# A decoder-layer kernel on one core: one level of Strassen on all projections but v and o

## The reference

```python
z = xn @ w_in                      # 1024 -> 7 * 1024: u, v, b_gate, c_gate, x_in, r_a, r_b
u, v = gelu(u), layer_norm(gelu(v))
y_a = (u * chunk_spatial_mix(v, w_s, b_s)) @ w_a_out
c_in = c_gate * x_in
y_b = (b_gate * short_conv(c_in, conv_w)) @ w_b_out     # causal, three taps
h = sigmoid(r_a) * y_a + sigmoid(r_b) * y_b
x1 = x + rms_norm(h @ w_o)
f = (silu(xn1 @ w_gate) * (xn1 @ w_up)) @ w_down        # xn1 = rms_norm(x1); hidden width 2816
y = x1 + rms_norm(f)
```

## Time and profile before

| | |
|---|---|
| median of 3 runs | 1787.79 us (1787.73 to 1787.82) |
| profiled execution: its own time | span 1785.2 us, from the first to the last instruction |
| TensorE, matmul (PE) | 1740.3 us, 97% of the span, 10888 matmuls |
| TensorE, weight loads (PEld) | 1712.0 us, 96% |
| VectorE (DVE) | 565.0 us, 32% |
| ScalarE (ACT) | 366.2 us, 21% |
| GpSimd (POOL) | 416.5 us, 23% |
| mean granted TensorE clock | 0.990 of 2.4 GHz |

### The profile page before, as it was taken

One profiled execution on the slowest core, in us unless ns is written; L12 is line 12 of the kernel. 1 busy time (PEld: TensorE's weight loads), 2 busy tenths in 40 slices (PEclk: granted clock), 3 DMA queues, 4 the chain that ended last, 5 costly groups with the idle time before them and its releaser, 6 DMA issues.

```text
span 1785.2 us, 25730 instructions
## 1 busy us (share of the span) xinstructions
PE 1740.3 (97%) x10888; PEld 1712.0 (96%) x10888; DVE 565.0 (32%) x720; ACT 366.2 (21%) x459; POOL 416.5 (23%) x211
## 2 busy tenths in 40 slices
PE   8999999999999999999888899999999999999997
PEld 6889999999999999999888899999999999999997
DVE  7645420001322322111446932122122122121225
ACT  5212211111111111111433321111111111111136
POOL 2001122222212122222644322222222112222215
PEclk9999999999999999999998999999999999999999
DMA  7221111111111111111330111111111111111102
GB/s 252 70 72 36 35 48 47 46 40 45 47 47 47 47 47 48 47 47 47 104 98 13 36 36 48 47 44 47 38 47 47 47 47 47 47 47 47 48 25 96
DMA packets 145598, 96.89 MB, mean 54 GB/s; under 512 B 5092, under 2 KB 136292, under 8 KB 145556
## 3 DMA queue, kind: packets, MB, share of 16 engines
q1 hardware_dynamic: 133808, 91.34, 16.6%
q10 hardware_dynamic: 11748, 4.95, 1.0%
HBM read 87.75 MB, written 8.56 MB: 54 GB/s over the span
## 4 chain that ended last, share of the span: by engine, by line
PE 91%; DVE 7%; ACT 2%; issue 0%; DMA 0%; DVEq 0%; POOL 0%; SPq 0%
PE ps L449 88%; DVE g L1332 1%; DVE tmp L1323 1%; PE ps L532 1%; DVE xt L1318 1%; DVE g L1317 1%; DVE tmp L1301 1%; PE ps L741 0%; PE ps L708 0%; DMA g<-in_w_in 0%; DVE op_lo L1112 0%; PE ps L623 0%; PE ps L479 0%; DVE xn_lo L1260 0%; ACT g L964 0%
## 5 line engine op out<-in xcount | busy, mean ns | idle before, releaser
L365 POOL TENSOR_TENSOR ring_lo<-stage,ring_hi 128x1024 fp32r<-128x1024 f32 x129 | 310.3, 2406 | 1228.7 <-ACT ring_hi L859 1226.6
L449 PE MATMUL ps<-xn_hi,ring_hi 128*128 128x344 f32 x2208 | 481.5, 322 | 3.9 <-DVE xn_lo L1341 3.2
L449 PE MATMUL ps<-xn_lo,ring_hi 128*128 128x344 f32 x2208 | 479.3, 320 | 0.9 <-issue 0.9
L449 PE MATMUL ps<-xn_hi,ring_lo 128*128 128x344 f32 x2208 | 477.7, 320 | 0.0
L449 PEld LDWEIGHTS ps<-xn_hi,ring_hi 128*128 128x128 f32 x2208 | 374.2, 188 | 4.9 <-DVE xn_lo L1341 3.5
L449 PEld LDWEIGHTS ps<-xn_lo,ring_hi 128*128 128x128 f32 x2208 | 375.7, 189 | 1.5 <-issue 1.4
L449 PEld LDWEIGHTS ps<-xn_hi,ring_lo 128*128 128x128 f32 x2208 | 371.1, 188 | 0.0
L449 PE MATMUL ps<-op_lo,ring_hi 128*128 (+3 forms) x1472 | 287.0, 318 | 0.4 <-DVE y_raw L1442 0.3
L859 ACT ACTIVATE ring_hi<-stage 128x1024 fp32r<-128x1024 f32 x124 | 131.0, 1057 | 656.4 <-PE ps L449 656.4
L449 PEld LDWEIGHTS ps<-op_lo,ring_hi 128*128 128x128 f32 x1472 | 241.4, 188 | 0.9 <-DVE y_raw L1442 0.5
L1387 DVE TENSOR_TENSOR tmp<-ps,tmp 128x1032 f32<-128x1032 f32 x20 | 24.7, 1233 | 391.1 <-PE ps L449 391.1
(11 more groups left out here) (174 smaller groups left out, 1329.7 us busy)
## 6 DMA issues: line engine op xcount, KB each, us to landing
stage<-in_w_in SPq DMA_DIRECT2D x48, 512.0 KB, 3.8
stage<-in_w_gate SPq DMA_DIRECT2D x22, 512.0 KB, 3.9
stage<-in_w_up SPq DMA_DIRECT2D x22, 512.0 KB, 3.9
stage<-in_w_down SPq DMA_DIRECT2D x22, 512.0 KB, 3.7
xt<-xt_dram SPq DMA_DIRECT2D x3, 1376.0 KB, 11.8
tmp<-in_x_prompt SPq DMA_DIRECT2D x8, 512.0 KB, 5.4
g<-in_w_in SPq DMA_DIRECT2D x8, 512.0 KB, 9.1
xt_dram<-tmp ACTq DMA_DIRECT2D x8, 512.0 KB, 4.3
```

Of the source, the lines that this page charges most:

```text
L365: pool.tensor_tensor(lo, src, hi.bitcast(f32), SUB).then_inc(w_lo, 1)
L449: ins = pe.matmul(o, w, xc, start=first and n == 0, stop=last and n == 2)
```

## The change

The kernel is written anew around one level of Strassen's scheme, in the form with seven products and few additions (Winograd's).

*Blocks.* The 1032 tokens form four quarters of 258 (256 prompt and 2 sample tokens; `CS`): two token halves b, each in two pieces gg. A *block* is two tiles of output channels over the whole contraction of 1024. It takes seven `product`s; each goes over 4 slices of the contraction (even or odd ones, or a sum of such), 3 matmuls, 2 pieces of 258 columns: 24 matmuls, 168 a block. There are 66 blocks: 4 of u, 12 of c, x, b, 4 each of r_a, r_b, a_out and b_out, 22 of gate and up, 12 of down, whose last four go over 3 slices instead of 4 (126 matmuls). The first u block is plain (192 matmuls), v stays as it was, o stays plain (768 matmuls of 258 columns). The sum is 192 + 61 x 168 + 504 + 768 = 11712 matmuls of 258 columns.

*Weights.* Each block is loaded whole (1 MB, stages in turn). VectorE forms 4 sums of quarters (`sums`, 128 x 512), ScalarE 7 hi parts (`hi`), GpSimd 7 lo parts (`rest`).

*Outputs.* The seven products land in four PSUM regions X, Y, Z, W of two banks, used twice: ScalarE copies one out (`s1`), VectorE does seven additions of 516 columns with one input in PSUM: c11, u1, u3, u2, c22, c12, c21. A product waits until its region is free: product 5 for c11, product 6 for u1, the next block's product 0 for u2, its product 1 for c22, 2 for c12, 3 for c21.

*Operands.* Seven of eight token `slots` hold the token side of the seven products, hi and lo, 2064 columns each: slots 0, 2 and 3 are quarters of the operand (even or odd slices, one token half), slots 4 to 7 sums of two to four quarters. When the operand changes (before a_out, before b_out, before down and twice inside it) a new *generation* has to be made in the same slots: 4 additions on VectorE (`t_add`), 7 hi parts on ScalarE (`t_split`), 4 lo parts on VectorE and 3 on GpSimd (`t_rest`), each over 2064 columns (1548 in the last). A slot may be overwritten only after its product in the last block of the old operand, and the product of the first block of the new operand waits for its slot. The first generation (of xn) is made after v (`tx_sum_of`, `tx_rest`), with three instructions for a sum; that of gate and up in two halves (`f_add`, `f_split`, `f_rest`), and the first gate block runs as two half runs of 258 tokens. SBUF has no room for all operands: the b product, the gates sigmoid(r_a) and sigmoid(r_b), and the hidden activations go to DRAM and come back (`tgen_load`, `gate_load`).

*Order.* The loops are unrolled. Half of the norms' work is placed anew: chunks of o are 258 tokens; `second_norm` stands after the sixth unit of the next chunk. x1 goes to DRAM after the norm and comes back at the end, where nothing of down is cut in pieces except the last block, which runs as two halves; `y_scale` then does each quarter's norm on 258 columns across the partitions.

The core of the diff (the file's other lines are the same stages in the new layout):

```diff
-            def unit(slot, grp, x_h, x_l):
-
-                out = [ps[:, 3 * grp + c, 0:CW] for c in range(CH)]
-                for k in range(KT):
-                    w = slice(128 * k, 128 * k + 128)
-                    ins = three(out, ring_hi[slot][:, w], ring_lo[slot][:, w], parts(x_h, k), parts(x_l, k), k == 0, k == KT - 1)
-                ins.then_inc(acc_full, 1)
+            def product(run, b, p, gs):
+                pe.wait_ge(w_lo, hi_at(b) + LO_AT[p])
+                if p == 4:
+                    pe.wait_ge(s1_done, run)
+                elif p == 5:
+                    pe.wait_ge(c11_done, run)
+                elif p == 6:
+                    pe.wait_ge(u1_done, run)
+                elif run > 1:
+                    pe.wait_ge((u2_done, c22_done, c12_done, c21_done)[p], run - 1)
...
+                r, s = PBANK[p], PSLOT[p]
+                outs = [ps[:, 2 * r + c, 0:CS] for c in range(gs.start, gs.stop)]
+                for kp in range(kps(b)):
+                    c = slice(128 * kp, 128 * kp + 128)
+                    ins = three(outs, ring_hi[:, p, c], ring_lo[:, p, c],
+                                *([tp[:, s, part, n, kp, 0:CS] for n in range(gs.start, gs.stop)] for part in range(2)),
+                                kp == 0, kp == kps(b) - 1)
+                ins.then_inc(prod_done, 1)
+            def fresh(n, p):
+                if p in (1, 4, 6):
+                    pe.wait_ge(t_lo_pool, 3 * n + (1, 4, 6).index(p) + 1)
+                else:
+                    pe.wait_ge(t_lo_dve, 4 * n + (0, 2, 3, 5).index(p) + 1)
...
+            def prepare(b, n=None, kp=MP):
+                rest(b, 0)
+                rest(b, 2)
+                rest(b, 1)
+                if n is not None:
+                    t_rest(n, 1, kp)
+                rest(b, 4)
+                rest(b, 3)
+                rest(b, 5)
+                if n is not None:
+                    t_rest(n, 4, kp)
+                rest(b, 6)
+                if n is not None:
+                    t_rest(n, 6, kp)
...
+            def t_end(n, r, kp):
+                t_add(n, 2, r, kp)
+                t_add(n, 3, r, kp)
+                for p in (2, 3, 5):
+                    t_rest(n, p, kp)
...
+            def y_scale(n):
+                b, gg = O_CHUNKS[n]
+                base, sq, inv_y, tmp = (t[:, :] for t in rsq)
+                dve.wait_ge(y_sum, n + 1)
...
+                dve.tensor_tensor(g[:, :, b, gg], g[:, :, b, gg], inv_y.unsqueeze(1).to_broadcast((128, KT, CS)), MUL).then_inc(y_scaled, 1)
...
+                dve.tensor_tensor(g[:, 0:5, b, gg], g[:, 0:5, b, gg], x1_out[n % 2][:, 0:5], ADD).then_inc(y_ready, 1)
```

More of the change, by code:

```diff
@@ L1082, in _ @@
+            act.activation(warm, eps, ACT.Sqrt)
+            s1(R_LAST + 1, only[1])
+            y_sqrt(0)
+            y_sqrt(1)
+            for e in range(16, 20):
+                sq_gain(e)
+            y_evict(0)
+            y_evict(1)
+            y_sqrt(2)
+            y_sqrt(3)
+            for u in range(2, 10):
+                y_evict(u)
         @block.vector
@@ new lines, in middle, with c_run @@
+            def middle(r, nb, dst):
+                u1(r)
+                u3(r, dst)
+                sums(nb, 1)
+                u2(r)
+            def c_run(r, mp):
+                sums(r + 1, 0)
+                for n in range(4):
+                    if mp:
+                        dve.wait_ge(ob_saved[n], 16 * mp)
+                c11(r, q[:, 0])
+                middle(r, r + 1, q[:, 1])
+                c22(r, q[:, 3])
+                sums(r + 1, 2)
+                c12(r, q[:, 1])
+                sums(r + 1, 3)
+                c21(r, q[:, 2])
@@ new lines, in gate_run @@
+            def gate_run(r, n):
+                last = r == B_A - 1
+                sums(r + 1, 0)
+                if last:
+                    dve.wait_ge(u_prod, 4 * MP)
+                    t_add(0, 0, r, MP)
+                for i in range(4):
+                    if n:
+                        dve.wait_ge(gate_saved[i], 16 * n)
+                    else:
+                        dve.wait_ge(ob_saved[i], 16 * MP)
+                c11(r, q[:, 0])
+                middle(r, r + 1, q[:, 1])
+                c22(r, q[:, 3])
+                sums(r + 1, 2)
+                if last:
+                    t_rest(0, 0, MP)
+                    t_add(0, 1, r, MP)
+                c12(r, q[:, 1])
+                sums(r + 1, 3)
+                c21(r, q[:, 2])
@@ L1451, in _ @@
-            c = len(PIECES) - 1
-            mean_square(c)
-            scales(c)
-            for y in range(*PIECES[c]):
-                finish(y, c)
+            f_add(0, 0)
+            f_add(0, 1)
+            x1(2)
+            f_rest(0, 0)
+            f_add(0, 2)
+            f_add(0, 3)
+            x1_squares_sum(2)
+            sums(B_F, 0)
+            f_rest(0, 2)
+            x1_norm(2)
+            sums(B_F, 1)
+            f_rest(0, 3)
+            sums(B_F, 2)
+            sums(B_F, 3)
@@ new lines, in _ @@
+            f_rest(0, 5)
+            r = B_F
+            x1(3)
+            dve.wait_ge(n_sum, 7)
+            c11(r, q[:, 0, 0:1], only[0])
+            u1(r, only[0])
+            u3(r, s_c[:, 0:1], only[0])
+            x1_squares_sum(3)
+            u2(r, only[0])
+            c22(r, s_b[:, 0:1], only[0])
+            c12(r, s_c[:, 0:1], only[0])
+            c21(r, s_b[:, 1:2], only[0])
+            x1_norm(3)
+            f_add(1, 0)
+            f_rest(1, 0)
+            f_add(1, 1)
+            f_add(1, 2)
@@ new lines, in _, with silu_run @@
+            f_add(1, 3)
+            for p in (2, 3, 5):
+                f_rest(1, p)
+            def silu_run(r, nb, gs):
+                sums(nb, 0)
+                c11(r, q[:, 0, gs], gs)
+                u1(r, gs)
+                u3(r, q[:, 1, gs], gs)
+                sums(nb, 1)
+                u2(r, gs)
+                c22(r, q[:, 3, gs], gs)
+                sums(nb, 2)
+                c12(r, q[:, 1, gs], gs)
+                sums(nb, 3)
+                c21(r, q[:, 2, gs], gs)
```

2633 lines of the change are left out of this document (1626 added, 1007 removed).

## The result

The changed kernel takes 1822.99 us (median of 4 runs, 1822.78 to 1825.27); the kernel before, on the same chip, 1787.76. The ratio is 1.0200, 95% interval 1.0186 to 1.0215: slower by 35 us, where 36 were forecast. The profiled execution has a span of 1821.3 us, at a mean granted clock of 0.948.

The account below looks back on a forecast made before the run. The prediction took TensorE's back-to-back matmuls as the bound; its terms, -180 - 6 + 100 + 18 + 25 + 47 + 6 + 26 = +36 on the profiled 1785.2, gave a median of 1824 us, range 1755 to 1880.

Parts of the forecast that it names:

- PE's own work: TensorE's matmuls over the whole kernel: 11712 of 258 columns at 118.7 ns, 1390 us instead of 1570, -180 us.
- first generation: Making the first operands after v: 14 long VectorE instructions in a 50 us queue delay TensorE, +18 us (10 to 25).
- convolution: Between x and b runs: two convolutions on VectorE delay c11, plus slow clock and late loads, four times, +25 us (5 to 35).
- five generations: Operand changes from a_out through down: VectorE and GpSimd SBUF work adds up and TensorE waits, +100 us (72 to 116).
- o to gate/up: From o's start to gate/up: waits for lo parts, norms and half runs, 86 us lost against 39, +47 (30 to 60).
- down's last blocks: In down's last blocks: exclusive VectorE and GpSimd work of 17.3 us against 14.9, +6 us (0 to 12).
- end: Behind the last product: VectorE's four quarters of 8.7 us each, gathers and store, 50 us against 24, +26 (20 to 33).
- Rival (d): TensorE's matmuls: narrow ones cost nearly what wide ones do, 158 ns whatever the width, 2284 us in all; chance 0.01.
- The v stage stays: At the start: the v stage is unchanged by the rewrite and ends near 130 us.
- The walk: Step-by-step count through VectorE's and GpSimd's alternating queues at the five generations: 106 us of waits, 116 with the slow clock.
- Rival (a): At the five generations: VectorE and GpSimd don't shut each other out in these forms, 1714 us; chance 0.12.
- Rival (b): At the generations: the walk is too strict, the sum bound of 72 us holds, 1739 to 1790 us; chance 0.21.

Follow-up runs that it names:

- the combined kernel: Changed kernel with all generation lo parts on VectorE, sample stores and second norm later, GpSimd wait at o, fourth mix earlier, end reordered: 1771.82 us, ratio to before 0.9914.

## Why the prediction was right, and which terms were off

| term | predicted | measured |
|---|---|---|
| PE's own work | -180 | -157 |
| bias, x1 transposes | -6 | -5 |
| start | 0 | +9 |
| first generation | +18 | +19 |
| convolution | +25 | +5 |
| five generations | +100 | +96 |
| o to gate/up | +47 | +44 |
| down's last blocks | +6 | 0 |
| end | +26 | +25 |
| sum on the span | +36 | +36 |

The sign and the mechanism held: what TensorE saves, the two engines that form its operands give back, at few places, and half of it at the five generations. That the total came out within 1 us is luck: four terms were 34 us too low (23 of them TensorE's own work, 9 the start) and five 34 too high (20 of them the convolution).

**PE's own work: the size was off.** The matmuls of 258 columns stand 120.5 ns apart. I put a straight line through 256 and 344 columns; at 256 the changed kernel has the line's 117.8. The step between 256 and 258 is three times the line's, and why is open. Down's last blocks have 120.0 ns. Rival (d) fell: narrow matmuls cost nearly in proportion.

**"The v stage stays": this step failed.** The list of what the change adds held four small stores on ScalarE's queue, and I gave them no price. Moving them won 9.2 us.

**The generations: the sum was right, its two parts were not.** The walk had 26, 29, 23, 19.7 and 18 with its 2 us of clock, the trace has 22.1, 27.3, 18.7, 15.1 and 13.0. The walk's waits were over-sized, 106 us where the trace has 73. The low clock behind them was under-sized, 10 us where it has 23; at o it was 8 for some 16. So the terms came out near in part because two errors cancel. The mechanism held. Rival (a) is excluded by the runs: VectorE's additions take 3.4 us beside GpSimd's work and 2.30 alone, one added wait halves the time of three lo parts, and GpSimd's lo parts cost less on VectorE. The Trainium skill (SBUF — State Buffer, Who interferes with whom) says that a VectorE instruction with two SBUF inputs contends with a GpSimd one that reads SBUF, that the shared ports are an exclusive lock, and that the order of issue decides who blocks. GpSimd's 3.93 us for two instructions of 128 columns agrees. Of the 96 us, 53 hang on the lo parts; the rest goes with the additions, which is read from the order and the stretched rows and was not tried apart.

**Convolution: over-sized.** The first output sum of a b run is ready 35.8 us after the start of the x run (forecast 38.6), and each of the four waits is 1.12 us long and costs 1.3. The stretches of slow clock and the late loads that I had added did not come: after so short a wait the blocks that follow are again 20.25 us.

**o to gate/up: right.** 19.8 us at the start of o (forecast 22), norms 4.5, 4.6 and 7.6 (5.4, 5.4, 9), then the half runs. That part of the start of o is exclusion, and not the length of VectorE's queue alone, is shown by the added wait.

**End: right**, 49 us for 50, though the six terms that I wrote for a quarter add up to 8.25 us and not to 8.7. **Down's last blocks: nothing lost.** TensorE has no wait from one to the next and takes 15.12 us for 126 matmuls, with GpSimd busy all the time and the block not held up:

```profile
1742.20:1757.30 15.10, 15.10 (x128) 15.10 (x127) 14.16 (x16) 8.50 (x16) 15.10 (x12) 1.00 0.16 66
```

Rival (b), that the walk was too strict, was wrong for the kernel as it stood; its point, that the losses are made of order as much as of work, is what the combined kernel uses: the same products, 51 us less.

## What to carry to other kernels

A scheme that trades matmuls for additions is paid for where operands change. Price those places by a walk through the queues of VectorE and GpSimd as one resource, by the number of instructions as well as by their length, and then put onto one engine, or behind a wait, what would alternate on two. Every DMA that a change adds gets a price on its issuer's queue, small ones too, above all where several of small pieces follow each other. Behind each wait, price the matmuls at the low clock. And when such a change comes out a little slower, look at the waits by place before giving it up: six edits of order and place turned +2.0% into -0.9%.

## What the runs showed of the hardware

- Four DMA issues of 8 KB in pieces of 8 bytes held ScalarE's queue for 10.57 us: the first two 0.60 and 0.75, the third 6.09, the fourth 3.03.
- After a wait of 4 us, 18 matmuls of 258 columns stood some 215 ns apart, at a granted clock of 0.50.
- Matmuls of 256, 258 and 344 columns stand 117.8, 120.5 and 158.0 ns apart: the two columns more cost 2.7 ns.
- A GpSimd instruction of 128 columns takes 2.0 us (mean of two) beside VectorE's long ones and at most 0.66 alone: short instructions don't slip between.
- Moving work can pay nearly as much as taking it away: the six edits that leave nothing out, at the generations and elsewhere, gained 51 us, all lo parts of the five generations cut to an eighth 56.
